# A hybrid attention layer on one core: turns at the head of each step, scores and minima together, projections last; the feed-forward loop written out

## What is computed

```python
def residual_tail(h, oa, ob, g_out_a, g_out_b, w_out, g_ffn, w_gate, w_up, w_down):
    mixed = jnp.concatenate([rmsnorm(oa, g_out_a), rmsnorm(ob, g_out_b)], axis=-1)
    h = h + mixed @ w_out
    u = rmsnorm(h, g_ffn)
    return h + (jax.nn.silu(u @ w_gate) * (u @ w_up)) @ w_down

def layer_prompt(h, rel_bias, g_attn, w_in, b_forget, sinks, g_out_a, g_out_b,
                 w_out, g_ffn, w_gate, w_up, w_down):
    u = rmsnorm(h, g_attn)
    qa, ka, va, logf, qb, kb, vb = project(u, w_in, b_forget)
    oa = fox_prompt(qa, ka, va, logf)
    ob = swa_prompt(qb, kb, vb, rel_bias, sinks)
    h = residual_tail(h, oa, ob, g_out_a, g_out_b, w_out, g_ffn, w_gate, w_up, w_down)
    return h, (ka, va, logf, kb[:, -WINDOW:], vb[:, -WINDOW:])
```

## Time and profile before

| what | us |
|---|---|
| median of 3 runs | 1540.81 (1539.42 to 1544.92) |
| the profiled execution | 1547.3 |
| its span, first to last instruction | 1545.5 |
| TensorE busy | 1439.7 |
| VectorE busy | 579.1 |
| ScalarE busy | 472.9 |
| GpSimd busy | 214.5 |

### The profile page before, as it was taken

The page is one execution under the profiler, slowest core; times in us unless marked ns, Lnnn a source line. Parts: engine busy times, 40 slices in busy tenths (PEclk is TensorE's granted clock), DMA queues, the critical chain, the costliest instruction groups (busy, mean ns, idle before and its releaser), DMA issues.

```text
span 1545.5 us, 23325 instructions
## 1 busy us (share of the span) xinstructions
PE 1439.7 (93%) x9041; PEld 1312.5 (85%) x9041; DVE 579.1 (37%) x1374; ACT 472.9 (31%) x1044; POOL 214.5 (14%) x317
## 2 busy tenths in 40 slices
PE   5988988899999977999999999998999999999996
PEld 3877877677777756887999989998999899999996
DVE  6235543323132343553324242433333234335155
ACT  6335453354544474343321112020211111121103
POOL 2125442252434241000000000000000000000000
PEclk9989999899999978999999999999999899999998
DMA  7611113111212043012221111111111111120002
GB/s 189 119 44 29 33 46 92 32 56 39 73 53 70 8 144 120 29 41 72 82 80 41 44 43 42 42 41 42 42 42 42 42 41 42 42 69 14 28 1 113
DMA packets 104690, 87.42 MB, mean 57 GB/s; under 512 B 14336, under 2 KB 95328, under 8 KB 104072
## 3 DMA queue, kind: packets, MB, share of 16 engines
q1 hardware_dynamic: 104584, 85.91, 19.4%
HBM read 71.10 MB, written 14.89 MB: 56 GB/s over the span
## 4 chain that ended last, share of the span: by engine, by line
PE 86%; ACT 5%; DVE 4%; issue 3%; DMA 1%; POOL 1%; SPq 0%; DVEq 0%; ACTq 0%
PE ps L530 27%; PE ps L531 25%; PE ps L532 25%; PE ps L723 2%; PE ps L848 2%; PE ps L689 1%; ACT sp_x L1132 1%; PE ps L735 1%; DMA out<-outb 1%; DVE ps L1476 1%; PE ps L636 1%; DMA out<-raw 1%; ACT ph_w L1103 1%; PE ps L651 1%; DVE raw L1723 0%
## 5 line engine op out<-in xcount | busy, mean ns | idle before, releaser
L1680 DVE TENSOR_TENSOR outs<-outs,ps 128x384 f32<-128x384 f32 (+1 forms) x264 | 134.5, 510 | 112.1 <-PE ps L532 112.0
L1665 DVE TENSOR_TENSOR gu<-ps,sg 128x384 f32<-128x384 f32 (+1 forms) x66 | 34.6, 525 | 260.6 <-PE ps L532 260.6
L1832 POOL TENSOR_TENSOR pl_x<-sp_x,ph_x 128x512 fp32r<-128x512 f32 (+5 forms) x120 | 102.1, 864 | 167.8 <-ACT sp_x L1132 166.2
L1295 ACT ACTIVATE h_hi<-gu 128x384 fp32r<-128x384 f32 (+1 forms) x66 | 32.9, 499 | 225.6 <-DVE gu L1665 225.6
L530 PE MATMUL ps<-f_hi,ff0hi 128*128 128x384 f32 (+1 forms) x264 | 89.3, 338 | 8.9 <-DVE ff4lo L1352 6.2
L1131 ACT ACTIVATE ph_x<-ps,negc 128x512 fp32r<-128x512 f32 (+5 forms) x120 | 63.2, 526 | 103.2 <-PE ps L735 103.2
L531 PE MATMUL ps<-f_lo,ff0hi 128*128 128x384 f32 (+1 forms) x264 | 88.8, 336 | 2.2 <-issue 2.2
L1289 ACT ACTIVATE sg<-ps 128x384 f32<-128x384 f32 (+1 forms) x66 | 30.5, 465 | 191.0 <-PE ps L532 191.0
L532 PE MATMUL ps<-f_hi,ff0lo 128*128 128x384 f32 (+1 forms) x264 | 88.2, 334 | 0.0
L530 PE MATMUL ps<-f_hi,ff3hi 128*128 128x384 f32 (+1 forms) x264 | 85.6, 324 | 0.0
L530 PE MATMUL ps<-f_hi,ff2hi 128*128 128x384 f32 (+1 forms) x264 | 85.6, 324 | 0.0
(11 more groups left out here) (290 smaller groups left out, 3817.4 us busy)
## 6 DMA issues: line engine op xcount, KB each, us to landing
raw<-in_w_gate SPq DMA_DIRECT2D x22, 512.0 KB, 5.4
raw<-in_w_up SPq DMA_DIRECT2D x22, 512.0 KB, 5.2
raw<-in_w_down SPq DMA_DIRECT2D x22, 512.0 KB, 4.1
raw<-in_w_in SPq DMA_DIRECT2D x14, 512.0 KB, 3.8
cb<-c_scratch SPq DMA_DIRECT2D x4, 1312.0 KB, 6.7
xt<-in_x_prompt SPq DMA_DIRECT2D x8, 512.0 KB, 4.0
out<-outb SPq DMA_DIRECT2D x16, 256.0 KB, 2.4
raw<-in_w_out SPq DMA_DIRECT2D x8, 512.0 KB, 3.6
```

The costliest lines, as they stand in the source:

```text
L1295: act.activation(h_hi[par][:, f, c0:c0 + n], gu[(f + c) % 2][:, 0:n], ACT.Copy).then_inc(S["g_hi"], 1)
L1665: dve.tensor_tensor(gu[(f + c) % 2][:, 0:n], bank(3 + c, n), sg[c][:, 0:n], ALU.mult)\
L1680: add = dve.tensor_tensor(y, y, bank(6 + o % 2, whole * P).rearrange("p (t m) -> p t m", t=whole), ALU.add)
L1832: pool.tensor_tensor(pl_x[at][0:rows, 0:n], sp_x[at][0:rows, 0:n], ph_x[at][0:rows, 0:n].bitcast(F32), ALU.subtract).then_inc(S["x_pl"], 1)
```

## The change

`make_schedule` gives the items other parts, and the engines' programs walk five parts. In a window step: part 0 `amw` and the key turn, then the scores; part 1 the minima; part 2 half the projection and behind it the output turn `otw`; then the second scores; part 3 the other half; the values; part 4 the turn of the first cached keys, in the last step. In a step of the forgetting attention: part 0 the turns of keys, cached keys and offsets (and the first values), then the scores; part 1 the minima; part 2 the whole projection share of the step and behind it `otx`; the values; part 4 what was part 3. The four feed-forward loops become Python loops, so that their bodies are written out with constants.

```diff
     for s in range(NWU + 2):
-        if s >= 2:
-            task(("w", s, 0), "otw", s - 2)
         if s + 1 < NWU:
             task(("w", s, 0), "amw", s + 1)
         if pending:
-            turned(("w", s), True)
-        project(("w", s, 1), FILL_W[s] // 2)
+            turned(("w", s, 0))
         if s + 2 < NWU:
             minima(("w", s, 1), "mw", s + 2)
-        project(("w", s, 2), FILL_W[s] - FILL_W[s] // 2)
+        project(("w", s, 2), FILL_W[s] // 2)
+        if s >= 2:
+            task(("w", s, 2), "otw", s - 2)
+        project(("w", s, 3), FILL_W[s] - FILL_W[s] // 2)
     assert not pending
-    task(("w", NWU + 1, 0), "fc", 0)
+    task(("w", NWU + 1, 4), "fc", 0)
     for v in range(-LEAD, NX + 2):
         j, i = v % NFU, v // NFU
-        if v >= 2:
-            c = {5: 0, 13: 1, 1: 2}.get(j)
-            if c is not None:
-                for h in range(2):
-                    task(("x", v, 0), "otx", (v - 2) // NFU, c, h)
...
-        n = FILL_X.get(v, 0)
-        project(("x", v, 1), n // 2 if v >= 0 else n)
         if seg_at(v):
             minima(("x", v, 1), "mx", *seg_at(v))
-        if v >= 0:
-            project(("x", v, 2), n - n // 2)
+        project(("x", v, 2), FILL_X.get(v, 0))
+        if v >= 2 and j in (1, 5, 13):
+            for h in range(2):
+                task(("x", v, 2), "otx", (v - 2) // NFU, {5: 0, 13: 1, 1: 2}[j], h)
...
             for s in range(NWU + 2):
+                items("w", s, 0)
                 if s < NWU:
                     window_scores(WB0[s])
-                items("w", s, 0)
                 items("w", s, 1)
+                items("w", s, 2)
                 if s < NWU and WB0[s + 1] - WB0[s] == 2:
                     window_scores(WB0[s] + 1)
-                items("w", s, 2)
+                items("w", s, 3)
                 if 1 <= s <= NWU:
                     window_values(s - 1)
+                items("w", s, 4)
 
             for v in range(-LEAD, NX + 2):
+                items("x", v, 0)
                 if 0 <= v < NX:
                     fox_scores(v)
-                items("x", v, 0)
-                items("x", v, 1)
-                items("x", v, 2)
+                for part in (1, 2, 3):
+                    items("x", v, part)
                 if 1 <= v <= NX:
                     fox_values(v - 1)
-                items("x", v, 3)
+                items("x", v, 4)
...
             pe.wait_ge(S["c_lo3"], 2 * TILES)
-            with pe.Fori(0, (FFQ - 3) // 2) as i:
+            for i in range((FFQ - 3) // 2):
                 for half in range(2):
                     gate_up(2 * i + 1 + half)
                     down(2 * i + half, half)
```

More of the change, by code:

```diff
@@ L182, in make_schedule, with turned @@
     pending = []
-    def turned(step, before):
+    def turned(place):
         i, kind, t0, count = pending[0]
         x = 3 * w_fox(i, 0 if kind == "fk" else 2) + (t0 + count - 1) // 3
-        if x in done and done[x][:2] != step and before:
-            task((*step, 0), kind, i, t0, count)
+        if x in done and done[x][:2] != place[:2]:
+            task(place, kind, i, t0, count)
             pending.pop(0)
@@ L195, in make_schedule @@
     pending += turns[:3]
+    keyed = 1
     for s in range(NWU + 2):
-        if s >= 2:
-            task(("w", s, 0), "otw", s - 2)
         if s + 1 < NWU:
@@ L221, in make_schedule @@
             pending += turns[6 * (i + 1):6 * (i + 1) + 3]
-        if pending and turned(("x", v), True) and not pending:
-            task(("x", v, 0), "fc", pairs_keyed[0])
-            pairs_keyed[0] += 1
+        if pending and turned(("x", v, 0)) and not pending:
+            task(("x", v, 0), "fc", keyed)
+            keyed += 1
         if j == NFU - 4 and v < NX - NFU:
@@ L228, in make_schedule @@
             task(("x", v, 0), "amx", i, 2)
-        n = FILL_X.get(v, 0)
-        project(("x", v, 1), n // 2 if v >= 0 else n)
         if seg_at(v):
             minima(("x", v, 1), "mx", *seg_at(v))
-        if v >= 0:
-            project(("x", v, 2), n - n // 2)
+        project(("x", v, 2), FILL_X.get(v, 0))
+        if v >= 2 and j in (1, 5, 13):
+            for h in range(2):
+                task(("x", v, 2), "otx", (v - 2) // NFU, {5: 0, 13: 1, 1: 2}[j], h)
         if j == 3 and 0 <= v < NX:
-            task(("x", v, 3), "amx", i, 1)
+            task(("x", v, 4), "amx", i, 1)
         if j == 0 and 0 < v < NX:
             for a in ((0, 4), (4, 4), (8, 1)):
-                task(("x", v, 3), "fv", i, *a)
+                task(("x", v, 4), "fv", i, *a)
     assert fill[0] == 8 * 3 * NW and not pending
     return at, tasks, held
-pairs_keyed = [1]
 PLAN, TASKS, HELD = make_schedule()
@@ L1323, in _ @@
             step(0, 0, down_before=False)
-            with act.Fori(0, (FFQ - 3) // 2) as i:
+            for i in range((FFQ - 3) // 2):
                 step(2 * i + 1, 1)
@@ L1613, in _ @@
                     groups_norm(0)
-                for part in range(4):
+                for part in range(5):
                     items("x", v, part)
@@ L1706, in _ @@
             step(0, 0, down_before=False)
-            with dve.Fori(0, (FFQ - 3) // 2) as i:
+            for i in range((FFQ - 3) // 2):
                 step(2 * i + 1, 1)
@@ L1823, in _ @@
                     window_lo(WB0[s] + 1)
-                weights_lo("w", s, 1)
                 weights_lo("w", s, 2)
+                weights_lo("w", s, 3)
             def fox_lo(v):
@@ L2022, in _ @@
             for s in range(NWU + 2):
-                for part in range(3):
+                for part in range(5):
                     after_tasks("w", s, part)
@@ L2077, in _ @@
                 ffn_load(1, x)
-            with sp_.Fori(0, (FFQ - 3) // 2) as i:
+            for i in range((FFQ - 3) // 2):
                 for half in range(2):
```

1 line of the change is left out of this document (removed).

## The result

The changed kernel takes 1505.20 us (median of 4 runs, 1504.06 to 1505.42); beside it the kernel before took 1542.87 (1539.42 to 1546.77). The ratio is 0.9754, 95% interval 0.9727 to 0.9781. The direction was right, and so was the larger part (the loop). The new order of the attention stages was forecast to cost 2.0 us; it gains some 18. The profiled execution took 1505.42 us, 41.9 less than that of before, for which the sum had said 22.2 less.

What follows compares the result with a forecast made beforehand. TensorE's own order of work and its waits were taken to set the time. Loop -24.2, window stage +5.5, stretch around the forgetting attention -3.5: -22.2 from 1540.8 gives 1518.6 us, range 1506 to 1531.

Steps and rivals of the forecast that it cites:

- The feed-forward loop: Looped feed-forward blocks: written out, 8 blocks of 70.20 us take 561.6 us instead of 585.8, 24.2 us less.
- the 5.0 us that were left over: Feed-forward loop: part of the 24.2 us put down to short gaps behind the back edge and register work before waits.
- back edge is not the cause: Rival, feed-forward loop: weight splits hold the iteration starts, so writing out saves 0 to 5 us; 1538 to 1543 us; 4 in 100.
- The window stage: 113 to 252 us: 13.0 us of old waits go, 18.5 us of new ones come, mostly output turns; 5.5 us lost.
- The small terms: Window stage: minima waiting for the copy 1.4 us, ScalarE's weight blocks 1.5, first step 0.7; 3.6 us left in all.
- bound of 11 lost: Window stage: worst case, every step's output turn waiting 1.7 us for VectorE's reductions.
- The rival in which the turn does not wait: Rival, window stage: reductions are done before the output turn, so 9.4 us gained instead of 5.5 lost; 1503.7 us; 8 in 100.
- The steps ahead of the scores: Nine steps before the first scores: 7.7 us of new minima waits less 5.2 us of old waits gone, 2.5 us lost.
- each landing is far ahead of its use except the one above: Around the forgetting attention: SP's moved stores and loads cause no waits except the late store behind the first value turns.
- The steps with scores: Forgetting attention from the first scores: 6.0 us of minima waits for cache keys go, as their copies run beside the scores.
- nothing changes: Forgetting attention: later value turns have scores and still wait for the same store and split, so no gain or loss.
- The rival of the clock: Rival, window stage: idles of 1.3 us per step bring the clock to 1.2 GHz, 69 us lost, 1587 us; 3 in 100.

Runs made afterwards that it cites:

- the pair of runs above: Kernel before with only TensorE's feed-forward loop written out, 1524.28 us; with only ScalarE's, VectorE's and SP's loops written out, 1543.91 us.
- otw_late: Changed kernel with the window stage's output turns moved behind the second half of the projection, just ahead of the values: 1490.02 us, ratio 0.9647.
- the store first: Changed kernel with one SP weight load issued behind the store of the first value tiles instead of ahead of it: 1502.13 us, ratio 0.9712.
- lead_fill_first: Changed kernel with the projection ahead of the minima again in the nine steps before the first scores: 1497.56 us, ratio 0.9694.
- split_again: Changed kernel with half the projection again between scores and minima in the steps with scores, turns in their new places: 1507.71 us, ratio 0.9767.
- minima_first: Kernel before with feed-forward loops written out and, in steps with scores, minima ahead of the whole projection, turns unmoved: 1532.43 us, ratio 0.9898.

## Why the forecast was off, step by step

**The feed-forward loop.** Right in every digit: 8 blocks of 70.20 us, 561.60 measured, -24.2. The stalls were TensorE's back edge, as the start behind the loop had suggested, and the lowered clock came from them: 1.00 with them gone. Of the 5.0 us that were left over, 2.2 were second idles behind two of the back edges. The rival "back edge is not the cause" is ruled out by the pair of runs above.

**The window stage.** Mechanism right, size too large: +0.8 against +5.5. A step of after, in the order that the prediction counted:

```profile
181.97 0.39 PE L647 MATMUL ps<-qw_hi,ks_hi 64*128 64x256 f32 x2
...
182.56 0.50 PE L632 MATMUL ps<-ks_hi,qw_hi 64*128 64x256 f32 x4
182.82 0.76 DVE L1488 TENSOR_TENSOR sp_w<-ps,bias_t 128x256 f32<-128x256 f32 x2 [3.37 <-PE ps L652]
...
185.10 0.14 DVE L1476 DVE_READ_ACCUMULATOR2_ANT small<- 128x1 f32 x1
185.30 0.61 PE L605 MATMUL ps<-ident,ot_w 128*32 128x128 f32 x4 [0.99 <-DVE small L1476]
```

The addition begins 0.85 us after the scores, as counted; the reductions end at 3.27 (3.4 counted); TensorE arrives at 2.34 (2.1 counted), so it waits 0.99, not 1.3. Over the stretch the turns wait 9.7 us in 12 places, not 14.9 in 14. The small terms came to 1.6 us (0.9 in one wait for ScalarE, 0.7 in two shorter ones) instead of 3.6. So the mis-sized terms are these two; that the ends differed by tenths in a place with 14 repeats made 5 us, and the small terms 2 more. By the waits alone the stage should even have gained 1.7 (11.3 for 13.0). It lost 0.8, since its busy time rose by 2.6 us (133.77 to 136.34 in the stretches of the table), a term that the prediction did not have; its cause was not followed up. The prediction's bound of 11 lost leaves out its own small terms: 14 x 1.7 + 3.6 - 13.0 is 14.4. The rival in which the turn does not wait is wrong about this kernel, but `otw_late` shows what it would have been worth: its stage, from the first key-bias turn to the first minima behind it, is 12.5 us shorter than the changed kernel's (154.1 to 141.6), so 11.7 shorter than before, where that rival had said 9.4.

**The steps ahead of the scores.** The failing sentence is "each landing is far ahead of its use except the one above". The wait behind the value turns was counted at 3.9 us from the old timeline, in which SP's store stood where it had stood; with the projection behind the minima, right ahead of the next step's turns, the weight load, which follows POOL's split, goes out 1.9 us later against the turns, and the store behind it 1.1 us later and close behind the load. 6.15 was measured, 3.0 with the store first: less than 3.9, so the store's place was the whole of this miss. The other new waits were 1.0 for the cache keys (1.1 counted) and 2.2 in three more (2.7). To this comes what the prediction kept only in its bounds: the clock falls in the long wait (it stayed at 1.00 in this stretch of `lead_fill_first`, whose longest wait is 1.5 us). TensorE worked at 1.2 GHz for 4.7 us behind it, worth 2.3 us:

```profile
270.01:274.70 4.69, 4.69 (x18) 4.22 (x19) 1.41 (x4) 0.00 (x0) 0.41 (x2) 0.50 0.11 31
```

**The steps with scores.** The cache-key waits of 6.0 us went, as counted, and 3.2 us of other turns waiting for ScalarE; but 4.6 us came in three places where the prediction had said of the later value turns that "nothing changes":

```profile
PE ps L685 <- DVE vw_lo L1416: 4.6, 3, 1.9
```
With smaller ones idle fell by 8.7 us. The failing step is the sentence that an edit is worth what it takes out of or puts into TensorE's queue, and that the queue was then read by its waits alone. The projection's place was taken to be free where nothing waits for it. It was not: a cut costs 0.39 us each time, some 13 us in all, and it stood in the profile as busy time, in the starts of consecutive rows. `split_again` and `minima_first` show it step by step. The second part is an estimate of 4.8 us of clock, within what kernels of one order differ by; the prediction had counted the clock as a gain in the loop and nowhere else.

**The rival of the clock.** The window stage idles about 1 us in 12 steps and was granted 1.00 (first table of stretches). The Trainium skill, "TensorE: Matmul & The Clock Gate", "A second HAM failure mode: psum-queue depth-cycling", says that frequent small idles between groups of matmuls make the clock go down and up again; with these waits the trace does not show it. The clock did fall in the wait of 6.15 us.

## What to carry to other kernels

Before moving a piece of work, look at the starts of consecutive matmuls at its old and its new place: if it takes in another number of rows than its neighbours, each cut is paid in busy time, which no list of waits shows. Two moves that look alike can need each other: the minima ahead of the projection bring 7.9 us of new waits with the turns in their old place, as much as they save, and 2.3 with the turns at the head, since the copies then come ahead of the exponentials and beside the scores. And when a task moves, follow what each queue issues with it and when (here a 256 KB store stands behind a 512 KB load in both kernels, and the load now goes out late), and ask of each wait that is filled which one comes next.

## What the hardware showed that had not been expected

- About 0.1 us at each of four places around a pair of changes between matmuls that take in 64 and 128 rows, 0.39 us a pair, with no idle shown.
- At each taken back edge of its loop TensorE idles 2.7 to 3.2 us, in seven of nine cases once more 3 to 5 us later (0.7 to 3.0 us; nine back edges in three kernels), and then works some microseconds at 1.2 GHz; back edges of ScalarE, VectorE and SP beside it cost TensorE 0.5 us a block.
- In one and the same stretch of one and the same order the time at 1.2 GHz differed between two kernels by 27 us (52.5 and 25.2), worth 10.7 us of span; a gain of a few us in such a stretch can't be read from one execution. In the changed order six kernels of seven spent 29.8 or 29.9 us there.
